# Three of eight expert passes run with 64 seats, high and low parts side by side in one stationary tile

## The chip, the cores and the metric

One core of one Trainium2 chip runs the whole kernel. The metric is device time in microseconds (us), the median of several executions; lower is better. Engine names are those of the profile: PE is the matrix engine, PEld its loading of the stationary operand, DVE the vector engine, ACT the scalar engine, POOL the GpSimd engine, SP the engine that issues most of the transfers.

## The reference, cut to what matters

Two layers of an encoder on 256 tokens of width 1024. Each layer mixes tokens in three branches and then has a channel mixer: layer 0 a dense SwiGLU, layer 1 a mixture of eight experts of which each token takes two. All is float32.

```python
D_MODEL, SEQ, N_EXPERTS, TOP_K, D_FF_EXPERT = 1024, 256, 8, 2, 3584

def swiglu(h, w1, w3, w2):
    return (jax.nn.silu(h @ w1) * (h @ w3)) @ w2

def moe_swiglu(h, w_router, w1, w3, w2):
    top_v, top_i = lax.top_k((h @ w_router), TOP_K)
    combine = ...                      # softmax of the two, put at the two experts
    out = jnp.zeros_like(h)
    for e in range(N_EXPERTS):
        out = out + combine[..., e:e + 1] * swiglu(h, w1[e], w3[e], w2[e])
    return out
```

512 choices (256 tokens, two each) fall on eight experts. With the inputs of this case, the reference's router gives experts 0 to 7 the counts 69, 65, 81, 44, 63, 45, 71 and 74.

## The kernel before

**Precision.** A float32 product is made of three products of a rounded format: operand high part times high part, high times low, low times high. A high part is a rounded copy (ACT writes `whi` from the landed weights `raw`), a low part is the rest (DVE subtracts, `wlo`). So each megabyte of weights, a piece of 128 partitions x 2048 floats, is read once by ACT (L1660) and once by DVE (L2219). There are 7 landing buffers (`RAW`) and only 3 buffers for the split parts (`SPLIT`): ACT may write the high part of piece n only when PE has done all products of piece n-3, and SP may load piece n only when DVE has made the low part of piece n-7.

**The expert stage.** It begins at about 696 us and fills the rest of the program. The tokens of an expert are put into 128 seats (`CAP`): rows of x, normalised and scaled (`rows_out`), are scattered by POOL with indirect transfers into `rows_by_slot` in DRAM, and each expert's 128 rows are loaded, transposed and split into `hselT` (high, low). An expert has 3584 hidden channels, in 7 blocks (`NM`) of 512. Per block there are six pieces: w1 in two halves, w3 in two halves, w2 in two halves. `up` multiplies the stationary 128 tokens (`hselT`) with 512 moving weight columns: 4 x 3 matmuls per half (L1142 for the high weights, L1146 for the low ones). `hidden_T` transposes the gated hidden values (L1159, four transposes), `down` uses them as the stationary operand for w2 (L1175, 12 matmuls per half). Thus 72 matmuls of 512 columns per block.

**Order.** It is written out by hand. PE runs, for block b: w1 of b, transposes of b-1, w3 of b, w2 of b-1. Call the six pieces of a block A, B (w1), C, D (w3), E, F (w2). ACT and DVE follow in an order computed from PE's order by `e_room`: a split is put ahead of another step if its buffer will be free by then. For ACT that is: high parts up to D; SiLU of w1's sum of block b into `sgv` (L1668); high part of E; high part of the transposed hidden values (`hidden_hi`, L1673); then F and the next block. For DVE: low parts up to E; low part of the transposed hidden values (`hidden_lo`, L2238); F; the product of SiLU and w3's sum (`hidden`, L2227); A of the next block. All engines take their instructions in order.

**Loop.** Expert 0's first block is a "head", then a loop of 7 iterations does experts 0 to 6 (and the first block of the next expert), then comes the written-out "last" expert 7, whose result is not stored but scattered by matmuls straight into `x_sb`. The results of the others go from PSUM to `y_slot` (ACT, L1731) and to `y_by_slot` in DRAM; POOL gathers them at the end. If an expert has more than 128 tokens, a flag makes all engines run eight more passes ("over").

**Dispatch.** Between the router and the first experts DVE works on small tiles of 128 x 16: top two, rank of each token in its expert, and then (L2192 to L2203) the seat number `slot_i` of each choice and the flag. Next it scales the rows (L2207) and only then makes the low parts of pieces 3, 4 and 5 of the expert stage (L1804).

**Transfers.** SP loads every piece of 1 MB by itself. A w2 piece is made of whole rows, 4 KB runs in DRAM; a w1 or w3 piece is 512 columns of 512 rows, 2 KB runs.

Of the kernel before, what the change touches and what calls it, by code (L numbers as in the profile page):

```python
# [42 lines left out]
CAP = 128  # L43
RAW = 7
# [16 lines left out]
def plan_psum(depth, heads, x_heads, fcd, nblk):  # L61
# [16 lines left out]
    for l in range(depth):  # L78
# [69 lines left out]
        else:  # L148
# [7 lines left out]
            def expert_banks(phase):  # L156

                order = []
                if phase in ("head", "over"):
                    order += [("rows", 0, 7), ("rows", 1, 6)] if phase == "over" else []  # L160
                    order += [("e1", 0, 0), ("e3", 0, 1)]
                for b in range(1, nblk if phase != "head" else 0):
                    order += [("e1", b, 0), ("eT", b - 1, 2)]
                    if phase == "loop" and b == nblk - 1:
                        order += [("rows", 0, 7), ("rows", 1, 6)]
                    order.append(("e3", b, 1))
                    if b == 1:
                        order += [("ey", 0, 4), ("ey", 1, 5)]
                if phase == "loop":
                    order += [("e1", 0, 0), ("eT", nblk - 1, 2), ("e3", 0, 1)]  # L170
                elif phase != "head":
                    order += [("eT", nblk - 1, 2), ("selT", 0, 3)] + [("scatter", n, n) for n in range(4)]
                return order

            for phase, times in (("head", 1), ("loop", 7), ("last", 1), ("over", 8)):
                start = list(used)
                for kind, n, bank in expert_banks(phase):
                    used[bank] += 1
                    groups[phase, kind, n] = Group(bank, used[bank])
                for kind, n, bank in expert_banks(phase):  # L180
                    groups[phase, kind, n].per = used[bank] - start[bank]
                for bank in range(8):
                    used[bank] += (used[bank] - start[bank]) * (times - 1)
# [41 lines left out]
def build(nc, x, mem, positions, g_mix, w_in, g_q, g_kv, w_uq, w_uk, w_uv, g_sg, w_s, b_s, g_mem,  # L225
# [10 lines left out]
    FD, FE, NE = dense_w1.shape[2], moe_w1.shape[3], moe_w1.shape[1]  # L236
# [10 lines left out]
    JOBS = NE * (-(-SEQ // CAP))  # L247
    QS, XS = QK ** -0.5, (BW // XH) ** -0.5
    steps = mixer_steps(H, XH)
    groups = plan_psum(DEPTH, H, XH, FCD, NM)  # L250

    with ExitStack() as ctx:
# [58 lines left out]
        rank = sb("rank", [P, T, JOBS])  # L311
# [55 lines left out]
        y_by_slot = nc.dram_tensor("y_by_slot", [JOBS, CAP, D], F32, kind="Internal").ap()  # L367
# [60 lines left out]
        slots_known = sem("slots_known")  # L428
        dispatched = sem("dispatched")
# [78 lines left out]
        def e_source(kind, b, half, e, shift=0):  # L508

            if kind == "w2":  # L510
                r0 = (b * BM + half * BM // 2) * P
                src = moe_w2[0, shift:, :, :][e, r0:r0 + BM // 2 * P, :]
            else:
                w = moe_w1 if kind == "w1" else moe_w3
                src = w[0, shift:, :, :][e, half * D // 2:(half + 1) * D // 2, b * BM * P:(b + 1) * BM * P]
            return src.rearrange("(k p) c -> p k c", p=P)


        def half_pieces(*blocks):
            return [(kind, b, half) for kind, b in blocks for half in range(2)]  # L520

        head_items = half_pieces(("w1", 0), ("w3", 0))
        mid_items = [i for b in range(1, NM) for i in half_pieces(("w1", b), ("w3", b), ("w2", b - 1))]
        items = {"head": head_items, "loop": mid_items + head_items + half_pieces(("w2", NM - 1)),
                 "last": mid_items + half_pieces(("w2", NM - 1)),
                 "over": head_items + mid_items + half_pieces(("w2", NM - 1))}
        PER_E = len(items["loop"])
        HEAD = len(head_items)
        assert PER_E % RAW == 0 and PER_E % SPLIT == 0 and len(items["over"]) == PER_E
        at = {phase: {key: i for i, key in enumerate(order)} for phase, order in items.items()}  # L530
        first = {"head": 0, "loop": HEAD, "last": HEAD + PER_E * (NE - 1), "over": PER_E * NE}
        assert first["last"] + len(items["last"]) == first["over"]
        for n in range(HEAD + EARLY):
            key = items["head"][n] if n < HEAD else items["loop"][n - HEAD]
            piece(("e", DEPTH - 1, n), RAW, e_source(*key, 0))
        e_base = [16 * sum(len(p[2]) for p in pieces if p[1] == s and p[0][0] != "e") for s in range(RAW)]

        def times(phase, j):

            return PER_E * j if phase in ("loop", "over") else 0  # L540

# [89 lines left out]
        def e_room(phase, kind, n):  # L631

            limit = marks[phase, kind, n][0]
            own = [marks["item", phase, i][0] for i in range(len(items[phase]))]
            if phase == "loop":
                own += [c + marks["item", phase, 0][1] for c in own[:EARLY]]
                return EARLY + sum(1 for i in range(EARLY, PER_E + EARLY) if own[i - SPLIT] < limit)
# [11 lines left out]
        def _(pe):  # L649
# [476 lines left out]
            def up(phase, kind, b_, j, rows=None):  # L1126
# [3 lines left out]
                for half in range(2):  # L1130
# [4 lines left out]
                    else:  # L1135
                        order = [(k, a) for k in range(4) for a in range(2)]
                        if rows is not None:
                            rows(half)
# [23 lines left out]
            def down(phase, b_, j, halves=(0, 1)):  # L1162

                if 0 in halves:
                    read(pe, (phase, "eT", b_), j)
# [1196 lines left out]
```

## Time and profile before

| what | value |
|---|---|
| median of 3 runs | 1662.2 us (1662.18 to 1662.34) |
| span of the profiled execution (first to last instruction) | 1660.5 us |
| PE busy | 1644.2 us, 99% |
| DVE busy | 1286.4 us, 77% |
| ACT busy | 1058.6 us, 64% |
| expert stage | from about 696 us to 1650 us |

The profile gives the profiled execution its span; a time of its own, measured from outside, is not among the numbers shown, so the median of the runs stands beside the span: it is 1.7 us above it. "Busy" of PE counts overlapping matmuls, so a full PE row says that PE always had something in hand, not that it ran at its peak. A share of the whole span mixes the first 696 us with the expert stage; the stages have to be read apart.

### The profile page before, as it was taken

How to read it: one execution, taken by the hardware profiler on the slowest of the kernel's cores; microseconds unless marked ns; L12 is line 12 of the kernel's file. 1: busy time of each engine (PE TensorE's matmuls, PEld its weight loads, DVE VectorE, ACT ScalarE, POOL GpSimd, SP SyncE). 2: the span in 40 equal slices, each digit the busy share in tenths (PEclk: the TensorE clock that was granted, in tenths of full speed). 3: DMA queues.
4: the chain of work that ended last, by engine and by line, in shares of the span. 5: the costliest groups of instructions: out<-in, count | busy, mean ns of one | idle time of the engine just before them, and what ended most of it. 6: DMA issues, size and time to landing. Idle time of an engine off the chain costs nothing.

```text
span 1660.5 us, 22803 instructions
## 1 busy us (share of the span) xinstructions
PE 1644.2 (99%) x8464; PEld 1397.3 (84%) x8464; DVE 1286.4 (77%) x1163; ACT 1058.6 (64%) x961; POOL 30.1 (2%) x57
## 2 busy tenths in 40 slices
PE   9999999999999999999999999999999999999997
PEld 8988889999899888788888888888888888888885
DVE  7575567555567747698888888988888888888997
ACT  6654445434465544577777777777777777777775
POOL 1000000000000000010000000000000000000100
PEclk9999999999999999999999999999999999999999
DMA  7753488885365444799999999999999999999994
GB/s 233 231 188 121 150 279 298 264 263 189 103 207 191 140 139 165 253 379 393 395 394 386 357 394 388 359 391 385 364 384 376 375 392 364 387 388 360 394 392 160
DMA packets 243426, 496.98 MB, mean 299 GB/s; under 512 B 8534, under 2 KB 64400, under 8 KB 243360
## 3 DMA queue, kind: packets, MB, share of 16 engines
q1 hardware_dynamic: 237360, 479.23, 80.3%
q0 software_dynamic: 2624, 8.45, 1.5%
q10 hardware_dynamic: 3376, 8.39, 1.3%
q8 instruction: 44, 0.72, 0.2%
q14 instruction: 22, 0.18, 0.0%
HBM read 476.64 MB, written 19.40 MB: 299 GB/s over the span
## 4 chain that ended last, share of the span: by engine, by line
PE 91%; DVE 3%; ACT 3%; issue 2%; DMA 1%; SPq 1%; DVEq 0%; POOL 0%; ACTq 0%
PE bank L1142 25%; PE bank L681 20%; PE bank L1175 19%; PE bank L1146 12%; PE bank L852 9%; PE bank L1159 1%; ACT whi L1423 1%; PE bank L671 1%; DVE wlo L1804 1%; PE bank L966 1%; DMA x_sb<-in_x 1%; DMA hn<-in_mem 1%; ACT pbuf L1558 0%; SPq L1297 0%; PE bank L938 0%
## 5 line engine op out<-in xcount | busy, mean ns | idle before, releaser
L2219 DVE TENSOR_TENSOR wlo<-raw,whi 128x2048 fp32r<-128x2048 f32 x328 | 748.2, 2289 | 108.1 <-ACT whi L1660 108.1
L1660 ACT ACTIVATE whi<-raw 128x2048 fp32r<-128x2048 f32 x328 | 627.8, 1918 | 177.5 <-PE bank L1146 93.7
L1804 DVE TENSOR_TENSOR wlo<-raw,whi 128x2048 fp32r<-128x2048 f32 (+3 forms) x121 | 259.3, 2148 | 175.8 <-ACT whi L1423 174.0
L1142 PE MATMUL bank<-whi,yT_hi 128*128 128x512 f32 x896 | 352.5, 396 | 0.0
L1142 PE MATMUL bank<-whi,yT_lo 128*128 128x512 f32 x896 | 347.4, 390 | 0.0
L1423 ACT ACTIVATE whi<-raw 128x2048 fp32r<-128x2048 f32 (+3 forms) x121 | 217.8, 1801 | 137.4 <-PE bank L681 100.5
L1146 PE MATMUL bank<-wlo,yT_hi 128*128 128x512 f32 x896 | 240.0, 390 | 0.0
L1146 PEld LDWEIGHTS bank<-wlo,yT_hi 128*128 128x128 f32 x896 | 168.2, 188 | 35.5
L1142 PEld LDWEIGHTS bank<-whi,yT_lo 128*128 128x128 f32 x896 | 168.3, 188 | 33.7 <-DVE yT_lo L2187 0.2
L1142 PEld LDWEIGHTS bank<-whi,yT_hi 128*128 128x128 f32 x896 | 168.3, 188 | 33.5
L1175 PE MATMUL bank<-whi,yT_hi 128*128 128x512 f32 x448 | 176.1, 393 | 0.0
L1175 PE MATMUL bank<-wlo,yT_hi 128*128 128x512 f32 x448 | 174.6, 390 | 0.0
L1175 PE MATMUL bank<-whi,yT_lo 128*128 128x512 f32 x448 | 174.5, 389 | 0.0
L681 PE MATMUL bank<-hT_hi,whi 128*128 128x256 f32 x464 | 131.4, 283 | 0.0
L681 PE MATMUL bank<-hT_hi,wlo 128*128 128x256 f32 x464 | 131.3, 283 | 0.0
L681 PE MATMUL bank<-hT_lo,whi 128*128 128x256 f32 x464 | 131.3, 283 | 0.0
L1175 PEld LDWEIGHTS bank<-whi,yT_hi 128*128 128x128 f32 x448 | 84.0, 188 | 25.2 <-issue 9.2
L1175 PEld LDWEIGHTS bank<-wlo,yT_hi 128*128 128x128 f32 x448 | 84.1, 188 | 17.9
L1175 PEld LDWEIGHTS bank<-whi,yT_lo 128*128 128x128 f32 x448 | 84.2, 188 | 16.1
L681 PEld LDWEIGHTS bank<-hT_lo,whi 128*128 128x128 f32 x464 | 89.0, 192 | 0.4
L681 PEld LDWEIGHTS bank<-hT_hi,whi 128*128 128x128 f32 x464 | 89.0, 192 | 0.4
L681 PEld LDWEIGHTS bank<-hT_hi,wlo 128*128 128x128 f32 x464 | 89.0, 192 | 0.0
(287 smaller groups left out, 2014.0 us busy)
## 6 DMA issues: line engine op xcount, KB each, us to landing
raw<-in_moe_w SPq DMA_DIRECT2D x336, 1024.0 KB, 7.4
raw<-in_w_in SPq DMA_DIRECT2D x36, 1024.0 KB, 5.2
raw<-in_dense_w SPq DMA_DIRECT2D x30, 1024.0 KB, 6.5
raw<-in_w_br SPq DMA_DIRECT2D x12, 1024.0 KB, 5.0
raw<-in_w_out SPq DMA_DIRECT2D x8, 1024.0 KB, 5.1
rows_by_slot<-qxT SPq DMA_DIRECT2D x15, 512.0 KB, 7.0
raw<-in_w_mkv SPq DMA_DIRECT2D x6, 1024.0 KB, 8.4
y_by_slot<-qxT SPq DMA_DIRECT2D x9, 512.0 KB, 7.7
```

What stands on the lines that cost most here:

```text
L671: ins = nc.tensor.matmul(bank, lhs(k), rhs(k), start=(k == 0), stop=(k == n - 1))
L681: ins = nc.tensor.matmul(bank, lhs(a, k), rhs(b, k), start=(start and k == chunks[0] and a + b == 0), stop=(stop and k == chunks[-1] and a ...
L852: ins = nc.tensor.matmul(bank, src(a, x0), w[b_][:, w0, :], start=(start and q + i == 0), stop=(stop and last))
L966: ins = nc.tensor.matmul(b[:, t * SEQ:(t + 1) * SEQ], qT[0:QK, h, tok(t)], kT[0:QK, h, :], start=True, stop=True)
L1142: nc.tensor.matmul(b[:, :], hselT[a][:, half, tok(k)], w[:, k, :], start=(half + k + a == 0), stop=False)
L1146: ins = nc.tensor.matmul(b[:, :], hselT[0][:, half, tok(k)], w[:, k, :], start=False, stop=(half == 1 and k == 3))
L1159: ins = nc.tensor.transpose(b[:, tok(c)], g32_m[:, tok(c)], ident[:, :])
L1175: ins = nc.tensor.matmul(banks[4 + n][:, :], gated_m[a][:, b_ % 2, tok(2 * half + c)], w[p][:, c, n * HALF:(n + 1) * HALF], start=(b_ + ha ...
L1423: nc.scalar.activation(whi[:, m % SPLIT, 0:floats(n)], raw[:, pieces[n][1], 0:floats(n)], ACT.Copy).then_inc(hi_ready, 1)
L1660: nc.scalar.activation(whi[:, (E0 + n) % SPLIT, :], raw[:, n % RAW, :], ACT.Copy).then_inc(hi_ready, 1)
L1804: V.tensor_tensor(wlo[:, m % SPLIT, 0:size], raw[:, pieces[n][1], 0:size], whi[:, m % SPLIT, 0:size].bitcast(F32), ALU.subtract).then_inc( ...
L2219: V.tensor_tensor(wlo[:, s, :], raw[:, n % RAW, :], whi[:, s, :].bitcast(F32), ALU.subtract).then_inc(lo_ready, 1)
```

## The change

Each expert pass gets a role, in the fixed order H L H L H L H H. A heavy pass (H) is as before. A light pass (L) takes an expert with at most 64 tokens. Its 64 seats leave half of the 128 columns of the stationary tile free, and there the low part of the same tokens is put: the tile holds 64 high columns and 64 low columns of each group. A matmul with the high weights then gives high x high in rows 0 to 63 and low x high in rows 64 to 127 at once; a second one with the low weights is added into both (rows 64 to 127 get low x low too). So 8 x 2 instead of 8 x 3 matmuls per weight matrix and block, and 8 instead of 12 per half of w2.

The two halves of rows must be added. For the hidden values this is done in `hidden_T`: ACT copies w1's sum (no SiLU yet) to `silu_m`, DVE copies w3's sum to `g32_m`, and eight matmuls with a matrix `fold` (ones at p and p+64) transpose and add in one step, four for each, of 64 columns. Then ACT makes the SiLU of the folded w1 part (`silu_t`), DVE multiplies it with the folded w3 part (`gated_t`), ACT rounds the product into the high columns (`hidden_hi`), and DVE subtracts into the low columns. For the result, `fold_result` runs two matmuls of 512 columns in the next pass, after its first w1 block, and ACT copies and stores (`store_result`).

Which expert has which position is worked out on the chip by DVE from the token counts; expert 0 is always first. The three with the fewest tokens get the light positions. SP reads the expert's number of a position from `order_i` and uses it in the address. `y_by_slot` and the zeroed rows in DRAM change size (24 zeroed blocks before, 24 after). If a light expert has over 64 tokens or a heavy one over 128, sixteen more passes are run.

The loop over experts is written out: PE, ACT, DVE and SP have all eight passes as straight code. The host lays out w1 and w3 so that a half block (512 rows x 512 columns) is contiguous, two 4 KB runs per partition.

```diff
+LIGHT = 64
+ROLES = "HLHLHLHH"
@@ e_source
+            w = moe_w1 if kind == "w1" else moe_w3
+            return w[0, :, b, half, :, :, :][e, :, :, :].rearrange("k p c -> p k c")
@@ PE, up
+                    if is_light(phase):
+                        order = [(k, 0) for k in range(4)]
@@ PE, hidden_T
+                if is_light(phase):
+                    for i, src in enumerate((silu_m, g32_m)):
+                        for c in range(BM):
+                            a = (i * BM + c) * LIGHT
+                            ins = nc.tensor.matmul(b[:, a:a + LIGHT], src[:, tok(c)], fold[:, 0:LIGHT],
+                                                   start=True, stop=True)
@@ PE, down
+                    terms = ((0, 0), (0, 1)) if is_light(phase) else ((0, 0), (1, 0), (0, 1))
+            def fold_result(p):
+
+                for n in range(2):
+                    read(pe, (p, "ey", n))
+                    b = claim((p, "yf", n))
+                    mark(nc.tensor.matmul(b[:, :], fold, y_slot[:, n * HALF:(n + 1) * HALF], start=True, stop=True),
+                         (p, "yf", n))
@@ PE, blocks
+                    if b_ == 1 and phase != "over" and phase and light[phase - 1]:
+                        fold_result(phase - 1)
@@ SP
+            expert = {0: 0}
+            for n in range(HEAD + EARLY, N_E):
+                p = e_items[n][0]
+                if p not in expert:
+                    sp.wait_ge(order_known, 1)
+                    expert[p] = sp.value_load(order_i[0:1, p:p + 1], min_val=0, max_val=NE - 1)
+                load_item(n, expert[p])
@@ ACT
+            def silu_folded(p, b_):
+
+                b = full(act, (p, "eT", b_))
+                nc.scalar.activation(silu_t, b[:, 0:BM * LIGHT], ACT.Silu).then_inc(silu_t_ready, 1)
+
+            def hidden_hi(phase, b_, j=0):
+
+                if is_light(phase):
+                    read(act, (phase, "eT", b_))
+                    nc.scalar.activation(by_slot(gated_m[0][:, b_ % 2, :])[:, :, 0:LIGHT],
+                                         gated_t.rearrange("p (c s) -> p c s", c=BM), ACT.Copy).then_inc(g_hi, 1)
+                    return
@@ ACT, blocks
                     e_hi(e_room(phase, "e1", b_), j)
+                    if is_light(phase):
+                        e_hi(e_room(phase, "eT", b_ - 1), j)
+                        silu_folded(phase, b_ - 1)
                     e_silu(phase, b_, j)
+                    if b_ == 1 and phase != "over" and phase and light[phase - 1]:
+                        store_result(phase - 1)
...
                     e_hi(e_room(phase, "eT", b_ - 1), j)
                     hidden_hi(phase, b_ - 1, j)
@@ DVE, before slot_i: load, key_e, pairs_e, order_e, pos_e, cap_e, hits_e, order_i
+            b = full(dve, ("most", l))
+            free(V.tensor_copy(load, b[:, 0:NE]), ("most", l))
...
+            link(V.tensor_reduce(order_f, hits_e, AX_X, ALU.add))
+            V.tensor_copy(order_i[:, :], order_f).then_inc(order_known, 1)
@@ DVE, hidden_lo
+                if is_light(phase):
+                    dve.wait_ge(silu_t_ready, light_block(phase, b_))
+                    free(V.tensor_tensor(gated_t, silu_t, b[:, BM * LIGHT:2 * BM * LIGHT], ALU.mult), (phase, "eT", b_))
+                    dve.wait_ge(g_hi, count)
+                    part = by_slot(gated_m[0][:, b_ % 2, :])
+                    V.tensor_tensor(part[:, :, LIGHT:2 * LIGHT], gated_t.rearrange("p (c s) -> p c s", c=BM),
+                                    part[:, :, 0:LIGHT].bitcast(F32), ALU.subtract).then_inc(g_lo, 1)
+                    return
```

## Rows read from the trace of the kernel before

**Rows 1.** Page, part 1: busy time, share of the span, number of instructions

```profile
PE 1644.2 (99%) x8464; PEld 1397.3 (84%) x8464; DVE 1286.4 (77%) x1163; ACT 1058.6 (64%) x961; POOL 30.1 (2%) x57
```

**Rows 2.** Busy by stretch, an expert stretch; last three: PE clock, DMA share, GB/s

```profile
1000.00:1100.00 100.00, 100.00 (x456) 82.10 (x455) 87.59 (x50) 75.45 (x52) 0.00 (x0) 1.00 1.01 377
```

**Rows 3.** Groups in 1000 to 1119 us: busy, mean ns | idle before, releaser

```profile
L2219 DVE TENSOR_TENSOR wlo<-raw,whi 128x2048 fp32r<-128x2048 f32 x43 | 98.2, 2289 | 15.1 <-ACT whi L1660 15.1
...
L1660 ACT ACTIVATE whi<-raw 128x2048 fp32r<-128x2048 f32 x43 | 82.3, 1919 | 23.5 <-PE bank L1146 12.7 <-PE bank L1175 10.0 <-ACT mv L1731 0.7
L1668 ACT ACTIVATE sgv<-bank 128x512 f32<-128x512 f32 x7 | 4.2, 599 | 5.8 <-PE bank L1146 5.8
```

**Rows 4.** Waits of PE from 700 us to the end: total, times, longest

```profile
PE bank L1229 <- issue: 0.2, 1, 0.2
```

**Rows 5.** Chain that ended last: start, us, piece; row transposes, two blocks of expert 7

```profile
1154.82 0.87 PE bank L1187 x8
...
1545.97 0.44 PE bank L1159 x4
...
1562.78 0.44 PE bank L1159 x4
```

**Rows 6.** Timeline within one expert block: start, us, engine, line, tiles, idle before

```profile
1006.37 0.68 DVE L2238 TENSOR_TENSOR yT_lo<-bank,yT_hi 128x512 fp32r<-128x512 f32 x1
1006.98 2.28 DVE L2219 TENSOR_TENSOR wlo<-raw,whi 128x2048 fp32r<-128x2048 f32 x1
...
1009.17 0.68 DVE L2227 TENSOR_TENSOR sgv<-sgv,bank 128x512 f32<-128x512 f32 x1
...
1009.77 2.29 DVE L2219 TENSOR_TENSOR wlo<-raw,whi 128x2048 fp32r<-128x2048 f32 x1
...
1012.86 0.39 PE L1142 MATMUL bank<-whi,yT_hi 128*128 128x512 f32 x1
...
1018.58 0.60 ACT L1668 ACTIVATE sgv<-bank 128x512 f32<-128x512 f32 x1 [0.88 <-PE bank L1146]
...
1019.08 1.91 ACT L1660 ACTIVATE whi<-raw 128x2048 fp32r<-128x2048 f32 x1
```

**Rows 7.** Groups by form, whole span: nearest rows of 256 and 64 columns

```profile
L671 PE MATMUL bank<-raw,pbuf 128*128 128x64 f32 x128 | 16.0, 268 | 0.0
...
L1449 ACT ACTIVATE hT_hi<-bank,cols 128x256 fp32r<-128x256 f32 x24 | 9.1, 496 | 5.1 <-PE bank L746 5.1
...
L2136 DVE TENSOR_TENSOR mT_lo<-pbuf,mT_hi 128x256 fp32r<-128x256 f32 x21 | 8.9, 425 | 0.7
```

**Rows 8.** Issues of the expert results' store, one per loop iteration: ns, first and last start

```profile
L1734 ACTq DMA_DIRECT2D y_by_slot<-mv x7: 357/357/376, 827.2 to 1541.4; - x7
```

**Rows 9.** Timeline of DVE: a 64-column link, then the dispatch before the first experts

```profile
17.63 0.20 DVE L1856 TENSOR_SCALAR qxT<-qxT 128x64 f32<-128x64 f32 x1
...
698.66 0.17 DVE L2192 TENSOR_SCALAR place<-logits 128x16 f32<-128x16 f32 x1
...
700.26 2.47 DVE L2207 SCALAR_TENSOR_TENSOR pbuf<-x_sb,rin,mkT 128x1024 f32<-128x1024 f32 x2
702.65 6.76 DVE L1804 TENSOR_TENSOR wlo<-raw,whi 128x2048 fp32r<-128x2048 f32 x3
```

**Rows 10.** Chain: high weights of piece 3; router matmuls of 256 columns

```profile
682.55 1.82 PE bank L1071 x8
...
704.59 1.81 PE bank L1142 x8
```

**Rows 11.** DMA queue of SP in 1000 to 1100 us, then 1600 to 1640 us: packets, MB, share

```profile
q1 hardware_dynamic: 15384, 36.66, 98.8%
...
q1 hardware_dynamic: 4881, 12.97, 84.5%
```

**Rows 12.** Busy by stretch at the end; columns as in rows 2

```profile
1649.00:1652.00 3.00, 1.21 (x4) 0.67 (x4) 3.00 (x5) 2.16 (x6) 0.00 (x0) 1.00 0.03 8
1652.00:1660.00 8.00, 0.00 (x0) 0.00 (x0) 4.16 (x16) 1.88 (x4) 0.00 (x0) 0.65 0.35 134
```

More of the change, by code:

```diff
@@ L175, in plan_psum, with give @@
[L175 to L183, printed above, removed]
+            def give(phase, kind, n, bank):
+                used[bank] += 1
+                groups[phase, kind, n] = Group(bank, used[bank])
@@ new lines, in plan_psum @@
+            start = list(used)
+            for n in range(2):
+                give("over", "rows", n, 7 - n)
+            for b in range(nblk):
+                give("over", "e1", b, 0)
+                give("over", "e3", b, 1)
+                give("over", "eT", b, 2)
+            for n in range(2):
+                give("over", "ey", n, 4 + n)
+            give("over", "selT", 0, 3)
+            for n in range(4):
+                give("over", "scatter", n, n)
+            for name, g in groups.items():
+                if name[0] == "over":
+                    g.per = used[g.bank] - start[g.bank]
@@ L246, in build @@
     C_GATE = C_XQ + BW
-    JOBS = NE * (-(-SEQ // CAP))
+    LAST = NE - 1
+    light = [r == "L" for r in ROLES]
+    HEAVY = NE - sum(light)
+    assert len(ROLES) == NE and SEQ <= LIGHT + 2 * CAP and not light[0] and not light[LAST]
+    OVER = 2 * NE
+    JOBS = NE + OVER
     QS, XS = QK ** -0.5, (BW // XH) ** -0.5
     steps = mixer_steps(H, XH)
-    groups = plan_psum(DEPTH, H, XH, FCD, NM)
+    groups = plan_psum(DEPTH, H, XH, FCD, NM, OVER)
     with ExitStack() as ctx:
@@ L519, in half_pieces @@
[L519 to L532, printed above, removed]
+                src = moe_w2[0, :, :, :][e, r0:r0 + BM // 2 * P, :]
+                return src.rearrange("(k p) c -> p k c", p=P)
@@ L633, in e_room, with light_block @@
             limit = marks[phase, kind, n][0]
[L634 to L637, printed above, removed]
-            return sum(1 for i in range(len(own)) if i < SPLIT or own[i - SPLIT] < limit)
+            start, end = (N_E, N_E + PER_E) if phase == "over" else (0, N_E)
+            i = start + SPLIT
+            while i < end and marks["item", i - SPLIT][0] < limit:
+                i += 1
+            return i
+        def light_block(p, b):
+            return sum(light[:p]) * NM + b + 1
         FINAL = ((1, 0, HALF), (1, HALF, D))
-        N_ZEROED = (JOBS - 1) + (JOBS - NE + 1)
+        N_ZEROED = JOBS
         block = ctx.enter_context(nc.Block())
@@ L1736, in _ @@
-            n_done = EARLY
+            for p in range(NE - 1):
+                blocks(p)
+                e_hi(e_room(p, "e3", NM - 1))
+                reached(act, (p, "e3", NM - 1))
+                rows_hi_part(p + 1)
+                e_hi(e_room(p + 1, "e1", 0))
+                if light[p]:
+                    e_hi(e_room(p, "eT", NM - 1))
+                    silu_folded(p, NM - 1)
+                e_silu(p + 1, 0)
+                e_hi(e_room(p, "eT", NM - 1))
+                hidden_hi(p, NM - 1)
+                e_hi(e_room(p, "ey", 0))
+                act.wait_ge(slots_moved, 32 * p + 16)
+                for n in range(2):
+                    b = full(act, (p, "ey", n))
+                    free(nc.scalar.activation(y_slot[:, n * HALF:(n + 1) * HALF], b[:, :], ACT.Copy), (p, "ey", n))
+                if not light[p]:
+                    store_result(p)
```

524 lines of the change are left out of this document (300 added, 224 removed).

## The prediction, made before the changed kernel was run

> **What bounds the kernel now.** First the busy shares: PE is at 99% [rows 1]. The shares mix stages, so next the stretch 1000 to 1100 us of the expert stage: PE 100, DVE 87.6, ACT 75.5 of 100 us, clock 1.00, 377 GB/s [rows 2]. Then who waits: from 700 us to the end PE shows one wait, 0.2 us [rows 4], while DVE's idle time is ended by ACT's high parts and ACT's by PE, which frees the split buffers [rows 3]. No row there names a transfer. PE bounds all eight experts. A block lasts 16.81 us in expert 7 [rows 5] (72 matmuls at 0.227 plus four transposes at 0.11); with 0.87 us of row transposes [rows 5] an expert in straight code is 7 x 16.81 + 0.87 = 118.5 us. In the loop it is (1541.4 - 827.2) / 6 = 119.03 us [rows 8], so the loop itself costs 0.49 us per pass.
>
> But DVE is close behind. Start to start its low part costs 2.19 us (1006.98 to 1009.17) and a 512-column step 0.61 (1006.37 to 1006.98) [rows 6]; I take 2.21, between this and the 2.235 of the back-to-back triple, (6.76 - 2.29) / 2 [rows 9]. A heavy block is then 6 x 2.21 + 2 x 0.60 = 14.5 us of DVE against 16.8 of PE. Taking work off PE can give at most 2.3 us per block before DVE ends last, unless the change lightens DVE. It doesn't: every weight is still split.
>
> **A light block on PE.** 48 x 0.227 = 10.9, and the eight folding matmuls at the 0.125 us of the 64-column group (16.0 / 128) [rows 7] 1.0: 11.9 us.
>
> **A light block on DVE and ACT.** Here a new round trip stands in DVE's way. DVE's order is: product `gated_t`, wait for ACT's rounding, subtract, low part of F, copy of w3's sum, A, B, C, D, E. ACT's is: rounding, then the high part of F. F's high part can't be earlier, as `e_room` puts it behind `hidden_hi`. From the start of the product:
> - product, 256 columns: 0.45. Not in the trace with a PSUM operand; bounds 0.425 [rows 7] and 0.68, the 512-column form [rows 6]; I stay near the 256-column row.
> - DVE to ACT 0.03, and ACT's rounding of 256 columns 0.42: bounds 9.1 / 24 = 0.38 (its group's busy time by count, overlaps taken off) and 0.496 [rows 7]; I take a value between.
> - F's high part starts some 0.1 before that ends (1018.58 + 0.60 against 1019.08) [rows 6], at 0.80, and takes 1.92 [rows 3]: 2.72. DVE starts F's low part at 2.76; the subtraction (0.4) lies inside this wait.
> - low part of F 2.21, copy 0.60, five low parts 11.05.
>
> Sum 2.76 + 2.21 + 0.60 + 11.05 = 16.6 us, against 16.8 before. So nearly all of PE's 4.9 us is turned into PE idle time: PE waits about 2.1 us for the subtraction before E and 1.9 us for the low part of F. Other waits I followed (C's buffer is free only after F's products: its high part is ready 0.9 us before DVE wants it) are met in a steady block. Bounds of a light block: 14.5 (six low parts, a copy and two half-size steps, no waiting) to 17.6 (both unknown steps at 0.68, and 0.5 more of waiting).
>
> **A light pass as a whole.** I follow DVE from its low part of the pass's first piece; PE begins that piece 3.09 us later (1009.77, 1012.86) [rows 6]. The first block, with the preceding heavy pass's last w2 block in it, has no round trip: 15.3 us, DVE's 14.5 and 0.8 of waits for high parts. Then ACT takes the heavy result out of PSUM and issues its store before C's high part (two copies of 0.5, issue 0.36 [rows 8], with the buffer wait behind them): 2.0. Seven light blocks 116.3, low parts of the next rows 1.2: 134.8; PE starts the next pass's second block 1.3 later, at 136.1. Before it is 3.09 + 8 x 16.81 + 0.87 + 0.49 = 138.9. Gain 2.8 a pass, 8.3 for three.
>
> **Unrolling.** Four loop passes (positions 0, 2, 4, 6) stay heavy: 4 x 0.49 = 2.0 us gained. The cost is more instruction fetch; the straight code of expert 7 ran without a PE wait [rows 4], so nothing is charged. SP reads a register seven times; seven landing buffers are 7 x 2.83 = 19.8 us of pieces, which covers it.
>
> **fold_result.** Two matmuls of 512 float32 columns. 256 columns cost 1.82 / 8 = 0.23 [rows 10], so 0.45 each, 0.9 a pass, in a PE-bound heavy pass: no cover. Behind it on ACT two copies, a wait and the store stand ahead of E's high part; E's low part, then the subtraction, come about 0.5 us later than PE wants E. 1.4 x 3 = 4.2 us lost (bounds 2.7 and 6).
>
> **Dispatch.** Before `slot_i` DVE gets 14 small operations. A 128x16 link takes 0.17 and 0.04 to the next, a 64-column one 0.20 and 0.03 [rows 9]: 6 x 0.20 + 8 x 0.24 = 3.1. The seat number has three more links, 0.6, casts and flag 0.4: 4.1 us. Now L2192 to L2203 start at 698.66 and L2207 at 700.26, and the low parts of pieces 3, 4, 5 at 702.65 [rows 9]. Piece 3's is done at 704.9; PE wants it after its eight high matmuls, at 704.59 + 1.81 = 706.4 [rows 10]. The slack is 1.5 us, so PE stalls 4.1 - 1.5 = 2.6, with the rounding 2.7; pieces 4 and 5 then come in time. That is lost for good, since PE is the bound there. Bounds: 1 us (links at 0.17) and 4. The scatter of rows starts 4 us later and is wanted some 50 us later: nothing. The eight memsets and the `fold` matrix on POOL are hidden; so are the changed small steps in expert 7.
>
> **4 KB runs.** No row has the stage waiting for data, so they give nothing in heavy passes. A light block at 16.6 wants a piece each 2.77 us (now 2.83). Fitting time per packet and per MB to the two stretches (0.988 x 1600 us for 36.66 MB in 15384 packets, 0.845 x 640 us for 12.97 MB in 4881) [rows 11] gives 0.033 us and 29.3 us, and a piece of 256 packets 2.45 us on 16 engines. That is an extrapolation; the other end is today's 2.83, which is delivered. I take it that transfers keep up.
>
> The Trainium skill (DMA: Bandwidth & Descriptors, Bandwidth) says that for DRAM to SBUF the memory side binds at about 358 GB/s per core. By it a light pass could not beat 45.1 MB / 358 = 126 us, and the change would give nothing. The trace disagrees: 377 GB/s over 100 us [rows 2].
>
> **The sum.** -8.3 - 2.0 + 4.2 + 2.7 = -3.4 us on the span of 1660.5, so 1657.1; the median of the runs lies 1.7 above the span: **1658.8 us**.
>
> **Rivals.**
> 1. *PE's clock falls in the light passes (slower).* PE would be busy 11.9 of 16.6 us, with two idle gaps of about 2 us per block. For it: late in the program PE has no work from about 1650.2, and the clock over 1652 to 1660 is 0.65, so it fell from 2.4 to 1.2 GHz near 1654.4, after some 4 us of idleness [rows 12]. Against it: 0.65 takes in only that long gap, and no gap of 2 us is there to judge by. At 1.2 GHz a light block is 48 x 0.453 + 8 x 0.24 = 23.7 us of PE, which passes 16.6 once about 40% of PE's light work runs low. With all of it low 21 x 7.1 = 149 us more; half of the blocks fully low, 75 more: 1733. Chance 0.12. The Trainium skill (TensorE: Matmul & The Clock Gate, A second HAM failure mode) has this: frequent short idle spells between groups of matmuls can make the clock swing. By that rule this rival is the case.
> 2. *The round trip is hidden (much faster).* If ACT's high part of F came without delaying DVE, a light block would be 14.6: 21 x 2.0 = 42 less, 1617. Against it: the written order of both engines. Half of it hidden: 1638. Chance 0.12.
> 3. *The round trip is longer (slower).* A light block of 17.3, from a late high part of C or slower strided steps, adds 0.7 x 21 = 15: 1673. It decides from 16.8 on, where a light block is no shorter than a heavy one. Chance 0.14.
> 4. *Transfers bind.* A piece each 2.83 us would make light passes as long as before: 1667. Chance 0.04.
> 5. *It doesn't do what it says.* With the counts 44, 45 and 63 all light experts fit, the last by one seat; one token routed otherwise in rounding could still fit. If not, sixteen passes of 119 us: over 3500. Chance 0.01.
>
> **Numbers.** My forecast (light block 16 to 17) 0.57, and within it 1649 to 1669. A change of 0.2%, 3.3 us, is about what can be told from none, and my sum lies on that edge: of the 0.57 I give 0.29 to faster, 0.18 to same, 0.10 to slower. Rival 2 adds 0.12 to faster; rivals 1, 3, 4 and 5 add 0.27 to slower, 0.04 to same. Faster 0.41, same 0.22, slower 0.37. Range 1638 to 1685: below it lies half of rival 2, above it most of rival 1.
>
> **What would show it.** Light passes near 116 to 117 us between stores, with PE idle released by DVE's low part and subtraction; the DVE wait for ACT's F about 1.5 us per light block, or none (rival 2); granted clock 1.00 (rival 1 falls) or less; one PE stall of 2.7 us near 706 us; no ACT wait for `raw`. I am wrong if light blocks are below 16.0 or above 17.2 us.

## The result and the profile after

The changed kernel takes **1665.05 us** (median of 19 runs, 1663.95 to 1666.49) against 1662.18 us before (19 runs, 1661.92 to 1662.68): ratio 1.0018, 95% interval 1.0012 to 1.0024. That is 2.9 us slower, where I had forecast 3.4 us faster. The profiled execution has a span of 1663.1 us, 2.6 above the 1660.5 of before.

The page of after, parts 1 and 3, answers to [rows 1] and [rows 11]: PE has lost 62 us of work and DVE none. The weights come in 180016 packets.

```profile
PE 1582.4 (95%) x8224; PEld 1332.9 (80%) x8224; DVE 1286.1 (77%) x1204; ACT 1054.5 (63%) x988; POOL 32.4 (2%) x69
...
q1 hardware_dynamic: 180016, 479.23, 78.5%
```

**The light block.** This is the timeline of DVE (start, us, engine, line, operation, tiles, idle before and what ended it) for one block of 16.5 us, from one copy of w3's sum (L2363) to the next:

```profile
894.38 0.68 DVE L2363 COPY sgv<-bank 128x512 f32<-128x512 f32 x1
894.98 11.09 DVE L2352 TENSOR_TENSOR wlo<-raw,whi 128x2048 fp32r<-128x2048 f32 x5
905.99 0.41 DVE L2377 TENSOR_TENSOR cT<-cT,bank 128x256 f32<-128x256 f32 x1
906.88 0.42 DVE L2380 TENSOR_TENSOR yT_hi<-cT,yT_hi 128x256 fp32r<-128x256 f32 x1 [0.48 <-ACT yT_hi L1749]
908.68 2.29 DVE L2352 TENSOR_TENSOR wlo<-raw,whi 128x2048 fp32r<-128x2048 f32 x1 [1.38 <-ACT whi L1727]
910.89 0.68 DVE L2363 COPY sgv<-bank 128x512 f32<-128x512 f32 x1
```

In the same block ACT and then PE:

```profile
906.43 0.42 ACT L1749 ACTIVATE yT_hi<-cT 128x256 fp32r<-128x256 f32 x1 [2.93 <-DVE cT L2377]
906.75 5.50 ACT L1727 ACTIVATE whi<-raw 128x2048 fp32r<-128x2048 f32 x3
```

```profile
907.36 0.50 PE L1231 MATMUL bank<-whi,yT_hi 128*128 128x512 f32 x1 [1.17 <-DVE yT_hi L2380]
...
911.12 0.47 PE L1231 MATMUL bank<-whi,yT_hi 128*128 128x512 f32 x1 [1.65 <-DVE wlo L2352]
```

The round trip is there as predicted: ACT stands 2.93 us for DVE's product, rounds it, only then makes the high part, and DVE stands 1.38 us for that. Copy to copy the block is 910.89 - 894.38 = 16.51 us, against 16.81 for a heavy one [rows 5].

**A pair of positions.** The eight row transposes (seven sets) are a mark once per position; the view of their line gives first and last start, of before (L1187) and of after (L1251):

```profile
L1187 PE MATMUL bank<-ident,cqkv x56: 272/273/273, 797.5 to 1512.5; 128*128 128x128 f32 x56
```

```profile
L1251 PE MATMUL bank<-ident,cqkv x56: 272/273/281, 803.1 to 1512.6; 128*128 128x128 f32 x56
```

After is 5.6 us late at the first and 0.1 to 0.2 at the last. In the timeline of after the first, third and seventh sets start at 803.08, 1039.38 and 1511.87, so a heavy and a light position take 236.3 us together, against 2 x 119.03 = 238.1 [rows 8]: 1.8 us gained per pair, 5.4 in three. So all of the loss arises outside of these six positions. Where, in the order of time:

*Before the experts, +1.4.* POOL, after, and DVE behind it:

```profile
236.06 0.20 POOL L1449 MEMSET cT<- 128x128 f32 x1 [46.81 <-PE bank L943]
236.41 1.94 POOL L1452 TENSOR_SCALAR_AFFINE_SELECT cT<-cT 128x128 f32<-128x128 f32 x3
238.53 1.08 POOL L1456 DMA_DIRECT2D hn<-in_mem  x2 [0.17 <-issue]
```

```profile
246.27 0.76 DVE L1924 TENSOR_SCALAR hn<-hn,rin 128x1024 f32<-128x1024 f32 x1 [3.18 <-DMA hn<-in_mem]
```

The fold matrix stands in POOL's queue ahead of the second load of `mem`, which was issued at 236.66 before. DVE then waited 0.76 us for it, now 3.18, and its next step on `x_sb` starts at 248.69 in place of 247.31.

*The dispatch, +4.6.* DVE and PE after, then the busy time by stretch (columns as in [rows 2]):

```profile
699.99 0.16 DVE L2296 COPY cT<-bank 128x8 f32<-128x8 f32 x1
...
705.80 2.47 DVE L2341 SCALAR_TENSOR_TENSOR pbuf<-x_sb,rin,mkT 128x1024 f32<-128x1024 f32 x2
708.20 6.68 DVE L1908 TENSOR_TENSOR wlo<-raw,whi 128x2048 fp32r<-128x2048 f32 x3
```

```profile
710.53 1.20 PE L1192 MATMUL bank<-wlo,yT_hi 128*128 128x512 f32 x4 [2.79 <-DVE wlo L1908]
```

```profile
712.00:715.00 3.00, 3.00 (x9) 2.30 (x8) 3.00 (x3) 1.74 (x1) 2.69 (x2) 0.51 0.83 270
715.00:718.00 3.00, 3.00 (x14) 2.47 (x13) 2.68 (x2) 1.84 (x1) 2.69 (x2) 0.92 0.99 382
```

From 698.66 to 702.65 before [rows 9], from 699.99 to 708.20 now: 4.2 us longer. PE stands 2.79 us for the low part, as forecast (2.7). What I had not forecast is the granted clock of 0.51 just behind it, the lower of the two levels (1.2 GHz): nine matmuls in 3 us where the next 3 us have fourteen. Of before, then of after, the transposes of the first block:

```profile
712.60 0.60 PE L1159 MATMUL bank<-ident,sgv 128*128 128x128 f32 x4
```

```profile
718.62 0.60 PE L1211 MATMUL bank<-ident,sgv 128*128 128x128 f32 x4
```

They start 6.0 us later, of which 1.4 came from earlier, 2.8 is the stall and 1.8 the rest, almost all of it the clock: from the end of the stall to the transposes are 8.1 us, and 6.5 in experiment 3, where the same stall is followed by no fall.

*Pass 0 -0.4, six positions -5.4, the last crossing -0.1.* The forecast for them was -0.5, -5.7 and nothing.

*Expert 7, +0.9, and the tail, +1.6.* Transposes of two blocks of expert 7 after, then DVE at the end, of before and of after:

```profile
1545.92 0.60 PE L1211 MATMUL bank<-ident,sgv 128*128 128x128 f32 x4
...
1563.58 0.60 PE L1211 MATMUL bank<-ident,sgv 128*128 128x128 f32 x4
```

```profile
1651.51 1.22 DVE L2336 TENSOR_TENSOR hn<-x_sb,mkT 128x1024 f32<-128x1024 f32 x1
```

```profile
1654.31 1.23 DVE L2497 TENSOR_TENSOR hn<-x_sb,mkT 128x1024 f32<-128x1024 f32 x1 [1.76 <-issue]
```

Between the two sets lie 17.66 us, 16.81 before [rows 5]. And DVE has a pause of 1.76 us ahead of the final scaling that no event ends; before, there was none.

The sum: 1.4 + 4.6 - 0.4 - 5.4 - 0.1 + 0.9 + 1.6 = +2.6, the difference of the spans.

### The profile page after: what moved, and what is told of

It reads as the page before. It is cut to its first block, busy times and chain, and to the rows that moved or that the text cites. A ratio compares the mean times of both kernels' runs of the same rounds, so it can differ in the third digit from the quotient of the medians.

```text
span 1663.1 us, 21020 instructions
## 1 busy us (share of the span) xinstructions
PE 1582.4 (95%) x8224; PEld 1332.9 (80%) x8224; DVE 1286.1 (77%) x1204; ACT 1054.5 (63%) x988; POOL 32.4 (2%) x69
## 3 DMA queue, kind: packets, MB, share of 16 engines
q1 hardware_dynamic: 180016, 479.23, 78.5%
## 4 chain that ended last, share of the span: by engine, by line
PE 65%; DVE 22%; ACT 6%; issue 4%; DMA 1%; SPq 0%; ACTq 0%; POOL 0%; DVEq 0%; POOLq 0%
PE bank L731 20%; DVE wlo L2352 16%; PE bank L1188 12%; PE bank L1231 12%; PE bank L902 9%; PE bank L1192 6%; ACT whi L1727 3%; ACT whi L1494 1%; PE bank L721 1%; DVE wlo L1908 1%; PE bank L1016 1%; PE bank L1211 1%; DMA x_sb<-in_x 1%; DVE sgv L2363 1%; DMA hn<-in_mem 1%
## 5 line engine op out<-in xcount | busy, mean ns | idle before, releaser
L1188 PE MATMUL bank<-whi,yT_hi 128*128 128x512 f32 x896 | 312.6, 397 | 0.0
L1192 PE MATMUL bank<-wlo,yT_hi 128*128 128x512 f32 x896 | 243.5, 394 | 4.1 <-DVE wlo L1908 2.8
L1231 PE MATMUL bank<-whi,yT_hi 128*128 128x512 f32 x448 | 180.1, 402 | 57.5 <-DVE wlo L2352 30.7
L1188 PE MATMUL bank<-whi,yT_lo 128*128 128x512 f32 x560 | 217.2, 391 | 0.0
L1231 PE MATMUL bank<-wlo,yT_hi 128*128 128x512 f32 x448 | 175.8, 392 | 0.0
L1188 PEld LDWEIGHTS bank<-whi,yT_lo 128*128 128x128 f32 x560 | 105.5, 189 | 21.3 <-DVE yT_lo L2291 0.2
L1231 PE MATMUL bank<-whi,yT_lo 128*128 128x512 f32 x280 | 109.0, 389 | 0.0
L731 PE MATMUL bank<-whi,mT_hi 128*128 128x512 f32 (+1 forms) x204 | 79.6, 390 | 0.1
```

What stands on the lines that cost most here:

```text
L731: ins = nc.tensor.matmul(bank, lhs(a, k), rhs(b, k), start=(start and k == chunks[0] and a + b == 0), stop=(stop and k == chunks[-1] and a ...
L1188: nc.tensor.matmul(b[:, :], hselT[a][:, half, tok(k)], w[:, k, :], start=(half + k + a == 0), stop=False)
L1192: ins = nc.tensor.matmul(b[:, :], hselT[0][:, half, tok(k)], w[:, k, :], start=False, stop=(half == 1 and k == 3))
L1231: ins = nc.tensor.matmul(banks[4 + n][:, :], gated_m[a][:, b_ % 2, tok(2 * half + c)], w[p][:, c, n * HALF:(n + 1) * HALF], start=(b_ + ha ...
```

## The experiments

Each was timed beside the kernel before (1662.2 to 1662.4 us in all three sessions); ratios are to it. Differences to after are those of medians, and uncertain by about 1 us. One more thing moves them: behind the stall of PE at the dispatch, the time to the first block's transposes is 6.5 us in the trace of experiment 3, 8.1 in those of after and 5, and 9.3 to 9.4 in those of 1, 2, 4, 7 and 8, because the granted clock falls for a different length of time. So what an edit elsewhere is worth is best read at the place of the edit.

**1. No light position.**

```
-ROLES = "HLHLHLHH"
+ROLES = "HHHHHHHH"
```

> All eight positions are heavy (ROLES = HHHHHHHH): the unrolled code, the new layout of the weights and everything else of the change stay, the 64-seat positions go. Theory A (the change lost on its fixed costs, and the light mode itself gives next to nothing): against straight heavy code the trace of after has 236.3 us per pair of a heavy and a light position, where 14 blocks of 16.81 and two crossings of 0.87 above a block give 237.1, so the light mode is worth 0.8 a pair and three pairs 2.4; this kernel takes about 1667, slower than after by 1 to 3 us. The heavy blocks take 16.81 throughout. Rival B (the light mode loses by its fold, its exit of 2.8 us and the clock, and the unrolling had paid): this kernel is faster than after, 1660 to 1663. Rival C (my prediction's count: light passes worth 2.8 a pass less a fold of 1.4, three times): slower than after by 4 us, 1669.

1667.23 us, ratio 1.0026 (1.0017 to 1.0035): 2.2 slower than after, in intervals that overlap; the traces decide. Its positions take 118.51 us each (row transposes at 804.69, 923.19 and so on to 1515.73). Two are 237.0, the mixed pair 236.3, a difference of 2.2 over the six. Theory A holds: the light mode as written is worth 0.7 to 0.8 us a pair, since what its blocks win is given back by the fold and at the crossings.

**2. The fold matrix behind the load of `mem`.** On POOL the two `dma_start` of `hn` are moved ahead of the memset and the three `affine_select`.

> POOL issues the second load of mem before it makes the fold matrix, otherwise as after. Theory: in after the memset and the three affine_selects of the fold matrix stand ahead of that load, VectorE waits 3.18 us for it instead of 0.76, and the row scales that follow come 1.4 us later; with the order turned the time falls by 1.4 us (1.2 to 1.6), to about 1663.7, and the wait for hn<-in_mem is near 0.8. Rival: the delay is made up before the dispatch by another wait (TensorE is the bound there); then no change, within 0.3.

1663.13 us, ratio 1.0004 (0.9995 to 1.0013): 1.9 faster than after. POOL and DVE there:

```profile
236.33 1.06 POOL L1450 DMA_DIRECT2D hn<-in_mem  x2 [47.05 <-PE bank L943]
```

```profile
243.86 0.75 DVE L1924 TENSOR_SCALAR hn<-hn,rin 128x1024 f32<-128x1024 f32 x1 [0.73 <-DMA hn<-in_mem]
```

The wait is back at 0.73 us, and the stall at the dispatch ends 1.8 us earlier (708.72 against 710.53). So 2.5 us of small work on an engine that is 2% busy cost the kernel 1.4 to 1.9 us.

**3. The round trip taken apart.** In light blocks ACT makes F's high part ahead of the rounding that waits for DVE.

```
                     e_silu(phase, b_, j)
+                    if is_light(phase):
+                        e_hi(e_room(phase, "e3", b_), j)
...
                 e_silu(p + 1, 0)
+                if light[p]:
+                    e_hi(e_room(p + 1, "e3", 0))
```

> In the 64-seat blocks ScalarE makes the high part of the third piece's expert weights ahead of hidden_hi instead of behind it, otherwise as after. Theory A (a light block is set by a round trip between ScalarE and VectorE: VectorE waits 1.38 us for that high part, ScalarE stands 2.93 us for the product cT): the wait of 1.38 goes, the block falls from 16.51 towards VectorE's own 15.1 us, 18 such blocks give 1.3 each, so 20 to 28 us less: 1637 to 1645. Rival B (transfers bind as soon as the round trip is gone; six pieces a block at 16.51 are 2.75 us a piece, at 15.1 they are 2.52, faster than any stretch of the two traces): the block stays at 15.9 to 16.4 and ScalarE begins to wait for raw pieces; 1655 to 1663. Rival C (the high part only changes places with the hidden's: cT's high part is now late by 1.2 us, VectorE waits for it and TensorE for the transposes): no change or slower, 1664 to 1672.

**1640.82 us**, ratio 0.9871 (0.9855 to 0.9886): 24.2 faster than after. DVE, then ACT, in one block:

```profile
898.85 0.42 DVE L2381 TENSOR_TENSOR cT<-cT,bank 128x256 f32<-128x256 f32 x1
899.75 0.43 DVE L2384 TENSOR_TENSOR yT_hi<-cT,yT_hi 128x256 fp32r<-128x256 f32 x1 [0.48 <-ACT yT_hi L1749]
900.09 2.28 DVE L2356 TENSOR_TENSOR wlo<-raw,whi 128x2048 fp32r<-128x2048 f32 x1
```

```profile
897.29 1.92 ACT L1727 ACTIVATE whi<-raw 128x2048 fp32r<-128x2048 f32 x1 [0.94 <-PE bank L1192]
899.30 0.42 ACT L1749 ACTIVATE yT_hi<-cT 128x256 fp32r<-128x256 f32 x1
```

ACT now makes the high part in the 2.93 us in which it used to stand; the rounding follows without a wait, and DVE's low part starts right behind its subtraction. The block is 15.06 us (878.36, 893.41, 908.46 in starts of the folding matmuls), and DVE's only pause in it is 0.48. That is a block bound by DVE. Theory A holds, B and C fall. The three pairs take 227.9, 228.6 and 228.6 us, 23.7 less than in after; in the second and third a short fall of the clock makes one block 16.66 instead of 15.87.

**4. The same with the old layout.** `e_source` slices `moe_w1` and `moe_w3` as before, and the host leaves them as they are.

> As the kernel with the early high part, and the up weights again in the layout of before, with runs of 2 KB. If the light block is there set by the engines and the new layout is worth nothing: the same time as that one, within 0.5 us. If 4 KB runs carry the faster light blocks: 2 KB runs cost it, and ScalarE waits for raw pieces; by the packets (237360 against 180016 for the same bytes) the up pieces would be some per cent slower, 0.1 to 0.2 us on each of 4 pieces in a block, 18 light blocks: 7 to 14 us slower than with 4 KB.

1644.22 us, ratio 0.9887 (0.9871 to 0.9902): 3.4 slower than with 4 KB runs by the medians, though the intervals overlap; the six positions take 688.1 us here and 685.1 there. The views of waits from 800 to 1500 us have this row here (total, times, longest), and none on raw pieces with 4 KB runs:

```profile
ACT whi L1728 <- DMA raw<-in_moe_w: 19.8, 31, 1.6
```

The inner blocks are still 15.05, those at the end of a pass up to 16.58. The layout is worth about 3 us, between the two theories (0.5 at most, and 7 to 14), and only once the blocks ask for it.

**5. The change with the old layout,** the same edit on after.

> As after, with the up weights again in the layout of before (runs of 2 KB). Theory: the transfers have slack in both traces (no wait for a raw piece), so the layout is worth nothing here: 1665, within 0.5 us of after, though with the early high part it was worth 3.4 us (1640.8 against 1644.2). Rival: the light blocks at 16.5 us already run at 2.75 us a piece, and some wait for raw comes up in them: slower by 1 to 3 us.

1666.36 us, ratio 1.0024 (1.0013 to 1.0035), overlapping that of after. The block times in its trace are those of after to 0.05 us. The theory holds: in this change the layout does nothing that can be measured.

**6. The chain of small operations spread.** The links to `order_i`, the slots, the flag and the two scaled rows become eight portions, and ACT loads the rows of the second expert one block later:

```
                     e_lo(e_room(phase, "e1", b_), j)
+                    chain_step(phase)
                     hidden_lo(phase, b_ - 1, j)
                     e_lo(e_room(phase, "e3", b_), j)
+                    chain_step(phase)
...
                     hidden(phase, b_, j)
+                    chain_step(phase)
```

> As after, but VectorE no longer does the chain of small operations (order of the experts, slots, flag) and the scaled rows in one stretch ahead of the low part that TensorE waits for: they stand in eight portions of at most 1.2 us between the operations of blocks 1 to 3 of expert 0, and the load of the second expert's rows one block later. Theory A (the stretch cost its 4.2 us of delay, of which TensorE stood 2.79, and the clock fell for 3.5 us after that stall, 1.9 more): the stall goes, the granted clock stays at 1.00 at 712 to 718, and the kernel takes 5 to 6 us less, 1659 to 1660. Rival B (the clock falls there for another reason): 2.8 to 4 less, 1661 to 1662.5, and the dip stays. Rival C (the portions delay low parts in blocks 1 to 3, where VectorE has some 2 us to spare in 16.81): the blocks of expert 0 take 17 to 18 us and the gain is lost; 1664 to 1667.

1662.68 us, ratio 1.0002 (0.9993 to 1.0011): 2.4 faster than after. Busy time by stretch where the clock had fallen, then PE's two waits in the blocks of expert 0:

```profile
712.00:715.00 3.00, 3.00 (x17) 2.51 (x16) 3.00 (x2) 2.25 (x3) 0.00 (x0) 1.00 1.04 425
```

```profile
736.91 0.50 PE L1231 MATMUL bank<-whi,yT_hi 128*128 128x512 f32 x1 [0.23 <-DVE yT_lo L2402]
...
754.92 0.50 PE L1231 MATMUL bank<-whi,yT_hi 128*128 128x512 f32 x1 [0.75 <-DVE yT_lo L2402]
```

Stall and fall of the clock are gone: the first block's transposes start at 713.80, 4.8 us earlier. But two later blocks take 17.51 and 17.85 us and give 1.7 back. A and C are both in it: the portions exceeded what DVE has to spare there (2.9 and 3.4 us in blocks 1 and 2).

**7. Expert 7 and the tail.** ACT's high parts come ahead of the flag's load; the branch on the flag and what is behind it are left out on all engines (so it doesn't compute overflow, of which this input has none).

```
+            e_hi(e_room(LAST, "e1", 1))
             act.wait_ge(flag_ready, 1)
...
-            with act.If(overflow > 0):
+            if False:
```

> As after, with two edits in the last expert: ScalarE makes the high parts of the next pieces before it waits for and loads the overflow flag, and the branches on that flag and all that is behind them are left out on every engine (it does not compute what would overflow; nothing does with this input). Theory: the first block of the last expert goes from 17.66 back to about 16.9 (0.8 less), VectorE's 1.76 us of no work ahead of the final scaling goes (1.6 less); together 2.4 less, 1662.6. Rival for the tail (the pause is the wait for the sum of squares or for something else that the trace puts down to no one): only the 0.8 comes, 1664.2, and the pause at the end stays. Rival for the block: last_choice on VectorE made it late, not ScalarE; then it stays at 17.6.

1663.86 us, ratio 1.0009 (1.0000 to 1.0018): 1.2 faster than after, half of what was expected, with an uncertainty as large as that. The trace shows both terms in full; what is missing in its span stands at the dispatch, where the fall of the clock took 1.2 us more than in after's. Transposes in expert 7, and DVE at the end:

```profile
1547.58 0.60 PE L1211 MATMUL bank<-ident,sgv 128*128 128x128 f32 x4
...
1564.57 0.60 PE L1211 MATMUL bank<-ident,sgv 128*128 128x128 f32 x4
```

```profile
1653.46 1.22 DVE L2498 TENSOR_TENSOR hn<-x_sb,mkT 128x1024 f32<-128x1024 f32 x1
```

The block is 16.99 instead of 17.66, and the pause is gone (from the start of the last four sums into `x_sb`, at 1650.83, to the final scaling are 2.63 us, in after 4.47). Experiments 9 to 11 tell the two edits apart: they have the first alone, their block is 16.98 to 17.01, and the pause of 1.65 to 1.77 us stays. So the pause belongs to the branch over the overflow code, which before was crossed without one. Whether it is the distance jumped or the fetch of what lies behind was not told apart.

**8. Three light positions in a row.** Experiment 3 with `ROLES = "HLLLHHHH"`.

> With the early high part of the third experiment, and the three light positions in a row (HLLLHHHH) in place of alternating. That kernel saved 9.2 us a light position against two heavy ones (118.55 each against a pair of 227.9), while its inner light blocks take 15.06 against 16.81, which is 12.2 over seven blocks. Theory: the 3 us between are the price of going in and out (17.42 and 17.3 for the blocks at the exit); two of three exits become crossings of light to light; 3 to 6 us less than with HLHLHLHH (1640.8), 1635 to 1638. Rival (transfers: alternating lets the pieces run ahead in the heavy positions, three light ones in a row at 2.51 us a piece use that up): ScalarE waits for raw in the second and third, inner blocks of 15.4 to 15.8; 1640 to 1645.

1641.47 us, ratio 0.9869 (0.9854 to 0.9884): no different from experiment 3. My theory falls, and so does the rival: inner blocks are 15.05 in all three positions, so the transfers keep up. The crossing from light to light costs as much as going in and out: the three blocks around it take 16.33, 16.77 and 16.39, 4.3 us above 15.05. DVE there:

```profile
952.50 0.42 DVE L2384 TENSOR_TENSOR yT_hi<-cT,yT_hi 128x256 fp32r<-128x256 f32 x1 [3.54 <-ACT yT_hi L1749]
```

It waits 3.54 us. ACT before it:

```profile
948.71 1.92 ACT L1727 ACTIVATE whi<-raw 128x2048 fp32r<-128x2048 f32 x1 [1.07 <-PE bank L1192]
950.53 1.06 ACT L1771 ACTIVATE mv<-bank 128x512 f32<-128x512 f32 x2
951.67 0.33 ACTq L1777 DMA_DIRECT2D y_by_slot<-mv  x1
```

The two copies of the folded result and the issue of its store stand ahead of the rounding and make up 1.5 us of the wait; most of the rest is a high part that ACT could begin only then, at 948.71, where in an inner block it is done when DVE's product is.

**9. The version the experiments point to.** Experiments 2 and 3, the first edit of 7, and the chain spread anew (with the later load of rows as in 6):

```
+            order_a()
+            order_b()
+            lo_parts(n_lo + 1)
+            order_c()
+            chain = [slots_a, slots_b, lambda: scaled(0), lambda: scaled(1), flag]
```

> The version that the experiments point to: the early high part of the third piece (21.6 to 24.2 us in the third experiment), the load of mem ahead of the fold matrix (1.9), ScalarE's high parts ahead of the flag's load (0.7), and the chain spread anew: the order of the experts is worked out in the two pauses of 2.48 and 1.35 us that VectorE has at 700 to 706 in the sixth experiment, and only slots, scaled rows and flag (5.3 us) stand in blocks 1 to 3 of expert 0, where VectorE has about 2 us to spare in each. Theory: the terms add, 24.2 and 1.9 and 0.7 and 4 to 5 for the chain: 1665.05 less 31, 1633 to 1636. Rival (they share a bound: once light blocks run at VectorE's or the transfers' pace, a start that is earlier is given back by waits for raw): 1637 to 1640.

**1634.05 us**, ratio 0.9829 (0.9816 to 0.9843): 28 us below the kernel before and 31 below after. PE has no wait in expert 0. DVE works out the order in pauses that it has anyway:

```profile
699.36 0.15 DVE L2301 COPY cT<-bank 128x8 f32<-128x8 f32 x1
...
701.97 2.29 DVE L1913 TENSOR_TENSOR wlo<-raw,whi 128x2048 fp32r<-128x2048 f32 x1 [0.37 <-ACT whi L1494]
...
705.62 4.49 DVE L1913 TENSOR_TENSOR wlo<-raw,whi 128x2048 fp32r<-128x2048 f32 x2 [0.49 <-ACT whi L1494]
```

**10 and 11. The repairs alone:** with eight heavy positions, and with the light mode as the change has it.

> The same three repairs (mem before fold, high parts before the flag, the chain spread anew) with eight heavy positions and no light one. It says what the light mode is worth in either form by comparison. From the first experiment (1667.23) less 1.9, 0.7 and 4 to 5: 1660 to 1661, so level with or 1 to 2 us below the kernel before, whose seven positions of 119.03 become 118.51. Rival (the unrolled code costs something that the repairs don't reach): 1662 to 1664.

> The three repairs with the light mode as the change has it (late high part). If the light mode so is worth 0.8 a pair, this is 2.2 to 2.4 us below the heavy kernel with the repairs, 1658 to 1659, which is faster than before by 3 to 4: my prediction's time, reached only once the terms that it left out are taken away. Rival: the repairs don't add; 1660 to 1662.

1660.21 us, ratio 0.9987 (0.9978 to 0.9996), and **1658.82 us**, ratio 0.9980 (0.9971 to 0.9989). So unrolling with the repairs is worth 2.0 us, and the light mode as written 1.4 more, with intervals that overlap. All three repairs together take 6.2 us off the change. In the trace of experiment 11 the first light position takes 116.77 us and the others 115.7, because the clock falls in its second block; PE, then the stretch behind it:

```profile
834.79 0.50 PE L1231 MATMUL bank<-whi,yT_hi 128*128 128x512 f32 x1 [2.02 <-DVE yT_hi L2402]
```

```profile
838.00:843.00 5.00, 4.45 (x12) 3.54 (x13) 5.00 (x4) 2.47 (x2) 0.00 (x0) 0.55 1.02 406
```

## Why the prediction was wrong

*The size and the place of the light mode: right.* The light block was put at 16.6 us, bound by DVE, and measured at 16.51; the round trip has the order and the waits that I wrote down, 1.38 us for F's high part. The pair with its fold was to gain 2.8 + 0.5 - 1.4 = 1.9 us and gained 1.8. Inside of that, two errors cancel: the folding is 16 instructions and takes 1.9 us in place of 1.0, which is hidden behind DVE, and the way out of a light position costs 2.8 us (blocks of 19.1 and 17.3 in place of heavy ones) rather than 1.4, which is made up by shorter blocks on the way in (15.9 and 15.2). Of what I had too small, 0.8 is `fold_result`: its two matmuls are four instructions and take PE 1.7 us (952.73 to 954.44) where I had 0.9. So that 1.8 came out is in part luck.

*The dispatch: the step was right, its price too small.* The stall came out at 2.79 us (2.7 forecast). I weighed a fall of the clock only for the light passes (rival 1), where it was short, and not behind the stall that I had worked out myself. It cost 1.8 us; experiment 6, without the stall, has no fall either.

*The sentence that failed: "The eight memsets and the `fold` matrix on POOL are hidden; so are the changed small steps in expert 7."* I looked at POOL's share of busy time and not at what is queued behind the new instructions. The `fold` matrix held up a load that DVE was waiting for already (experiment 2: 1.9 us). In expert 7 ACT's load of the flag had come to stand ahead of high parts that PE needs (experiment 7: 0.67 of the 0.85 us that its block is too long).

*A term that I left out: the tail.* 1.6 us for the branch over an overflow body (experiment 7). I charged nothing for the straight code, on the ground that it ran without PE waits.

Together: 1.4 + 1.8 + 0.9 + 1.6 = 5.7 us of the 6.0 between forecast (-3.4) and result (+2.6); the rest is small differences in the other terms. Experiment 11, where all but the tail are taken away, takes 1658.82 us, the predicted time; since it also has no stall, that agreement is in part an accident.

*Rival 2 was the thing to see.* I had put the gain of hiding the round trip at 42 us and gave it 0.12 because the written order forbids it. The order could be changed by two calls, and gave 24: a block fell by 1.45 us, not by 2.0, as DVE still waits 0.48 us for ACT's rounding (its own work is 15.06 - 0.48 = 14.6, the figure of rival 2), and the blocks at the crossings gain less (18.2 to 17.4). Rival 1 came only in small: PE idles in gaps of 1.2 and 1.7 us in every light block, and the clock is 1.00 over 890 to 922 us. The Trainium skill (TensorE: Matmul & The Clock Gate, A second HAM failure mode) would have it swing there; in after's passes one short dip shows (0.83 over 840 to 850), which costs no block time, and in experiments 3 and 11 such dips cost 0.8 to 1.1 us in a light position. Rival 4 did not come either: 15.06 us for six pieces are 2.51 us a piece, and the page shows up to 409 GB/s in the slices of experiment 3. The Trainium skill's page HBM Reference (Specifications) says that a core streaming alone goes well above the per-core share that I had quoted, to about 425; the traces agree with that, not with 358. One figure of mine was off as well, with nothing resting on it: a pass is 42 pieces, 44.0 MB, and not 45.1.

## What to carry to other kernels

When a mode takes work off the bounding engine, first write out the order in which the next engine waits; a wait between two in-order engines (ACT 2.93, DVE 1.38 us) is often undone by moving one independent operation ahead of it, and here that was worth 24 us, where the whole change had moved 3. An instruction on an idle engine is free only if nothing behind it in that queue is already awaited: look at the queue, not at the share. Put a chain of small operations into the pauses that the timeline shows, in portions no longer than these.

## What was not expected of the hardware

- Behind one stall of PE of 2.79 us, which ends at 710.53, the granted clock is 0.51 over 712 to 715 in after. Over 710 to 721 it is 0.69 to 0.84 in after and in experiments 1, 2, 4, 5, 7 and 8. In experiment 3, with the same stall (2.79 us, ending at 710.81), it is 1.00 over 709 to 721. So a stall of this length costs clock in some executions and not in others (0 to 2.9 us, by the time to the next transposes), which may be why after's runs spread over 2.5 us and those of before over 0.8 (that link is not shown). Behind the idle gap of 2.0 us in the second block of a light position it is the same: the clock falls there in after (0.50 over 842 to 845) and not in experiment 5, with the same gap.
- A pause of 1.6 to 1.8 us on DVE behind a branch not taken over long code, with nothing in the trace that ends it; and a pause of 1.58 us on ACT (the 0.33 of a store's issue in it) at the load of a flag into a register, with the flag known since 705.9.
- Packets of 4 KB in place of 2 KB: 57344 fewer packets for the same 479.23 MB, worth nothing that shows at 2.75 us a piece, and about 3 us in all at 2.51.
